# A four-layer block in fp32: the decay levels of two layers moved to one engine, their steps and a compression product placed anew

## The chip, the cores and the metric

One of the eight cores of a Trainium2 chip runs the whole program. The metric is the device time of one execution in microseconds; before, three runs gave a median of 1442.73 us (1440.99 to 1444.5). The core has five engines that work side by side and wait for each other by semaphores: TensorE (PE, with PEld for its weight loads), VectorE (DVE), ScalarE (ACT), GpSimd (POOL), and SyncE (SP), which only starts DMAs here.

## The reference, cut to what matters

The input is 256 tokens of 1024 features, all in fp32. Two layers of a first model (a recurrent one, a forgetting attention) are followed by two layers of a second, called layers 2 and 3 below, which the change touches. Such a layer does

```
proj = rms_norm(h) @ w_in                       # hq hf hi hg nq, six k/v of 128, 24 gates
o_hg  = hgrn2(hq, hf, hi, hg)                   # 4 heads of 128
o_nsa = gated sum of three attentions of 8 heads of 64 (2 key heads):
        compressed keys (15 blocks), "selected" and sliding-window
h += concat(o_hg, o_nsa) @ w_out
h += (silu(g) * u) @ w_ffn_out                  # g, u = rms_norm(h) @ w_ffn_in
```

With 256 tokens the selected and the window attention are both plain causal attentions. `hgrn2` needs, for each head, the sum over earlier tokens s of q_t * k_s * (product of the gates f between s and t), times v_s. The compressed keys and values are silu(window of 32 tokens @ w1) @ w2, for keys and for values.

## The kernel before

**Weights.** Every large product is a stream of units: 128 x 1024 values, 512 KB, loaded by SyncE into one of 8 `raw` buffers. ScalarE converts a unit to a high part `whi` (`splits`, line 939), VectorE subtracts it to get the low part `wlo` (line 1516), and TensorE forms each product as three matmuls, high x high, low x high, high x low (`products`, lines 277, 281, 282). There are 4 split buffers, so both engines run at most 3 units ahead (`AHEAD`). Where an engine does other work it first catches up: `full(name)` (lines 942 and 1519) does `splits(fills[name].pos + AHEAD)` and then waits for the PSUM bank; `pos` is the unit count when that bank's fill was closed. In VectorE's `soft`, `cap` limits this to what the next scores will allow.

**Banks.** PSUM has 8 banks. `fill(name, bank)` waits until the bank's previous fill was read, `close` signals that it is full, `read_out(name)` waits for its reader.

**Order.** It is written out by hand. In layers 2 and 3 the front is: block A and B (key and value rows), `hf` by feature, `hq` by feature, the `nq` block (queries of the attentions), with `rows_turned` (turned keys and queries) and first levels hung behind single units; then four units of `windows_by_unit(0)` (the compression's first product, for keys, bank 0) and the last turns. Then `attend` runs 12 steps. Step n of TensorE does, in this order:

```
between[n]; scores(n+1); weave; between[(n,1)]; turns(n); weave; between[(n,2)]; values(n-1)
```

A weave is half a unit of product from `side()`: `windows_by_unit(1)` (values, bank 1), then `hi` and `hg` (banks 0 and 1), 20 halves in all, so steps 10 and 11 have none. Turns go to bank 6. ScalarE's `soft` in step n does its `between[n]`, then `exps(n+1)` and then the copy of turn n out of bank 6. VectorE's `soft` in step n does the row maximum of scores n (line 1601, scaled at 1605; ScalarE's exps(n) waits for it), then its `between[n]`. A step has 4 heads in the first two steps of each attention and 2 heads in the other four.

**The levels.** The gate products between s and t are built by doubling. Level 0 is the diagonal (`level(0, half)`, `diagonal`). Level l (1 to 7) pairs blocks of 2^(l-1) tokens, level 8 the two halves of the sequence. Before, there are four arrays of 128 x 1024: F (prefix products of the gates within a block), S (suffix products), K and Q. GpSimd updates S and F for each level (lines 1488 and 1489); VectorE's `advance(l)` forms X from K*S and Q*F (lines 1984 and 1985); TensorE multiplies (`level`, lines 735, 751, 742, bank 7), and VectorE takes the result under a mask (`take`, line 1965). Levels 0 to 2 stand in the front, levels 3 to 8 in steps 0 to 5. `hgrn_out` multiplies the finished matrix with the values.

**The compression.** `hidden_in(kv)` (ScalarE) and `ch_silu(kv)` (VectorE, line 1994) apply silu and free the bank; `ch_turned` turns the result (bank 6), `cmp_keys_values` is the second product (lines 784 and 786, bank 6), GpSimd's `cmp_key_rows` normalises the keys, `cmp_keys_turned` turns them (bank 6); then `cmp_scores`, `cmp_exps`, `cmp_probs`, `cmp_out`, `cmp_add`.

Of the kernel before, what the change touches and what calls it, by code (L numbers as in the profile page):

```python
# [86 lines left out]
def program(nc, a):  # L87
    ctx = ExitStack()
    with ctx:
# [150 lines left out]
        def _(pe):  # L240
# [139 lines left out]
            def windows_by_unit(kv, flat):  # L380
# [3 lines left out]
                out = fill(name, kv)  # L384
# [328 lines left out]
            for L in (2, 3):  # L713
# [11 lines left out]
                def level(l, half=0):  # L725

                    q, kk, X = slot(8, 1024), slot(1, 1024), slot(9, 1024)
                    name = f"lev{L}.{l}"
                    if l == 0:
# [3 lines left out]
                        for h in range(4):  # L733
                            c = h * T + half * P
                            m = pe.matmul(out[:, h * P:(h + 1) * P], kk[:, c:c + P], q[:, c:c + P], start=True, stop=True)
# [4 lines left out]
                    if l == LEVELS:  # L740
                        for h in range(4):
                            m = pe.matmul(out[:, h * P:(h + 1) * P], X[:, h * T:h * T + P],
                                          X[:, h * T + P:(h + 1) * T], start=True, stop=True)
# [3 lines left out]
                    for tt in range(TT):  # L747
                        for h in range(4):
                            c = h * T + tt * P
                            q2 = X[:, c:c + P].rearrange("p (n two m) -> p n two m", two=2, m=s)[:, :, 1, :]  # L750
                            m = pe.matmul(out[:, (tt * 4 + h) * 64:(tt * 4 + h + 1) * 64], X[:, c:c + P], q2,  # L751
# [3 lines left out]
                def hgrn_out(tt):  # L755

                    if tt == 0:
                        for t in range(TT):
                            read_out(f"hi{L}.{t}")
                        read_out(f"lev{L}.{LEVELS}")  # L760
# [49 lines left out]
                def cmp_out(tt):  # L810
# [3 lines left out]
                    out = fill(f"co{L}.{tt}", 3)  # L814
# [17 lines left out]
                def side():  # L832

                    yield from windows_by_unit(0, flat)
# [12 lines left out]
                def rows_turned(groups):  # L847

                    for g in groups:
                        pe.wait_ge(ev("zrow"), 2 * i + (1 if g == 2 else 2))  # L850
                        for tt in range(TT):
# [4 lines left out]
                            turn(f"zT{L}.{tt}.{g}", (6, 3)[tt], tiles)  # L856
# [1401 lines left out]
```

## Time and profile before

| | us |
|---|---|
| median of 3 runs | 1442.73 |
| the profiled execution | 1444.79 |
| its span, first to last instruction | 1443.0 |
| TensorE busy | 1359.7 (94%) |
| VectorE busy | 880.3 (61%) |
| ScalarE busy | 714.2 (49%) |
| GpSimd busy | 192.4 (13%) |
| mean granted TensorE clock | 0.97 |

The profile is one execution. Busy is time in which an engine ran an instruction. The chain that ended last is 81% TensorE, 10% VectorE, 5% ScalarE. The granted clock is the share of TensorE's full clock (2.4 GHz) that it was given; 0.50 is 1.2 GHz. A releaser, in brackets behind a row, is what ended the idle time before it. Matmul rows overlap, since the engine is pipelined; what one costs is read from the distance of starts. Layer 2's front and attention lie at 656 to 834 us, layer 3's at 1048 to 1226.

### The profile page before, as it was taken

The numbers are of one execution on the slowest core, as the hardware profiler recorded it, in microseconds if no ns is written. First come the engines' busy times: TensorE is split into PE (matmuls) and PEld (weight loads), VectorE is DVE, ScalarE is ACT, GpSimd is POOL, SyncE is SP. The second block draws the span as 40 slices with busy tenths as digits, with TensorE's granted clock in tenths as the row PEclk, the third lists the DMA queues.
The fourth block names the chain that finished last, engine by engine and source line by source line (L and its number), as shares of the span: only waits on it lengthen the run. The fifth ranks groups of instructions, "written<-read, shape, count | busy, mean of one in ns | idle before, by whom it ended". The sixth has DMA issues, their size and how long they took to land.

```text
span 1443.0 us, 18641 instructions
## 1 busy us (share of the span) xinstructions
PE 1359.7 (94%) x7251; PEld 1152.2 (80%) x7251; DVE 880.3 (61%) x1136; ACT 714.2 (49%) x1167; POOL 192.4 (13%) x206
## 2 busy tenths in 40 slices
PE   7879999999988999999989899999999898999998
PEld 5657888878777888888977778888888776788887
DVE  4875665665534656557764556666577555566665
ACT  6464554454454545446443345555464444455553
POOL 2211000011530300002322010000023220100000
PEclk9989999998999999999979999999999799999999
DMA  9333655544522555545431135555454311355551
GB/s 364 136 117 117 233 174 207 188 152 158 177 72 71 178 203 178 202 159 195 160 118 59 59 117 204 190 176 183 155 194 158 117 59 44 131 190 179 199 194 56
DMA packets 62328, 224.44 MB, mean 156 GB/s; under 512 B 7192, under 2 KB 7328, under 8 KB 62240
## 3 DMA queue, kind: packets, MB, share of 16 engines
q1 hardware_dynamic: 59616, 214.23, 42.7%
q0 software_dynamic: 1904, 6.82, 1.5%
q10 hardware_dynamic: 720, 2.19, 0.4%
q8 instruction: 58, 0.95, 0.3%
q14 instruction: 30, 0.25, 0.1%
HBM read 222.16 MB, written 1.05 MB: 155 GB/s over the span
## 4 chain that ended last, share of the span: by engine, by line
PE 81%; DVE 10%; ACT 5%; issue 3%; POOL 2%; DMA 0%; POOLq 0%; DVEq 0%; ACTq 0%
PE ps L277 15%; PE ps L281 15%; PE ps L282 15%; PE ps L323 15%; PE ps L327 7%; PE ps L423 3%; PE ps L458 2%; PE ps L330 2%; PE ps L481 2%; DVE wlo L1516 2%; PE ps L751 1%; ACT scr L993 1%; PE ps L329 1%; DVE xn L1555 1%; DVE small L1601 1%
## 5 line engine op out<-in xcount | busy, mean ns | idle before, releaser
L1516 DVE TENSOR_TENSOR wlo<-raw,whi 128x1024 fp32r<-128x1024 f32 (+1 forms) x402 | 485.7, 1229 | 295.3 <-ACT whi L939 293.7
L939 ACT ACTIVATE whi<-raw 128x1024 fp32r<-128x1024 f32 (+1 forms) x409 | 424.3, 1048 | 332.9 <-PE ps L323 178.6
L323 PE MATMUL ps<-XT,whi 128*128 128x512 f32 x896 | 318.6, 399 | 0.0
L327 PE MATMUL ps<-XT,wlo 128*128 128x256 f32 x896 | 251.7, 281 | 0.0
L323 PEld LDWEIGHTS ps<-XT,whi 128*128 128x128 f32 x896 | 168.5, 188 | 41.0
L277 PE MATMUL ps<-whi,HT_hi 128*128 128x512 f32 (+1 forms) x496 | 189.9, 383 | 6.8 <-DVE wlo L1516 6.3
L282 PE MATMUL ps<-whi,HT_lo 128*128 128x512 f32 (+1 forms) x496 | 188.4, 380 | 0.0
L281 PE MATMUL ps<-wlo,HT_hi 128*128 128x512 f32 (+1 forms) x496 | 188.0, 379 | 0.0
L327 PEld LDWEIGHTS ps<-XT,wlo 128*128 128x128 f32 x896 | 169.4, 189 | 1.2
L277 PE MATMUL ps<-whi,XT 128*128 128x512 f32 (+2 forms) x352 | 143.1, 407 | 16.7 <-DVE wlo L1516 7.9
L281 PE MATMUL ps<-wlo,XT 128*128 128x512 f32 (+2 forms) x352 | 137.8, 391 | 0.0
L282 PE MATMUL ps<-whi,XT 128*128 128x512 f32 (+2 forms) x352 | 137.2, 390 | 0.0
L277 PEld LDWEIGHTS ps<-whi,HT_hi 128*128 128x128 f32 x496 | 94.9, 191 | 24.5 <-DVE wlo L1516 7.9
L282 PEld LDWEIGHTS ps<-whi,HT_lo 128*128 128x128 f32 x496 | 95.0, 192 | 17.3
L281 PEld LDWEIGHTS ps<-wlo,HT_hi 128*128 128x128 f32 x496 | 95.1, 192 | 16.9
L993 ACT ACTIVATE scr<-ps,small 128x256 f32<-128x256 f32 (+1 forms) x96 | 47.4, 501 | 112.8 <-DVE small L1605 99.0
L1336 POOL TENSOR_SCALAR small<-small 128x1 f32<-128x1 f32 x20 | 11.0, 550 | 660.0 <-ACT xn L976 659.8
L277 PEld LDWEIGHTS ps<-whi,XT 128*128 128x128 f32 x352 | 70.5, 200 | 35.2 <-DVE wlo L1516 11.1
L277 PE MATMUL ps<-whi,MX_hi 128*128 128x512 f32 x192 | 79.2, 413 | 15.2 <-issue 6.1
L282 PEld LDWEIGHTS ps<-whi,XT 128*128 128x128 f32 x352 | 70.6, 201 | 13.6
L281 PEld LDWEIGHTS ps<-wlo,XT 128*128 128x128 f32 x352 | 70.8, 201 | 10.1
L282 PE MATMUL ps<-whi,MX_lo 128*128 128x512 f32 x192 | 76.6, 399 | 0.0
(253 smaller groups left out, 1933.6 us busy)
## 6 DMA issues: line engine op xcount, KB each, us to landing
raw<-in_w_m SPq DMA_DIRECT2D x152, 512.0 KB, 4.2
raw<-in_w_n SPq DMA_DIRECT2D x108, 512.0 KB, 4.2
raw<-in_w_c SPq DMA_DIRECT2D x48, 512.0 KB, 4.0
raw<-in_w_o SPq DMA_DIRECT2D x32, 512.0 KB, 3.5
raw<-in_w_kv SPq DMA_DIRECT2D x16, 512.0 KB, 4.1
raw<-in_w_b SPq DMA_DIRECT2D x16, 512.0 KB, 3.2
raw<-in_w_w SPq DMA_DIRECT2D x16, 512.0 KB, 4.2
raw<-in_w_a SPq DMA_DIRECT2D x12, 512.0 KB, 8.2
```

The lines of the kernel that those rows point to most:

```text
L277: m = pe.matmul(out, xh, wh, start=first, stop=False)
L281: pe.matmul(out, xh, wl, start=False, stop=False)
L282: return pe.matmul(out, xl, wh, start=False, stop=last)
L323: m = pe.matmul(outs[f][:, :], hi[:, j, at], both, start=(k == 0), stop=False)
L327: pe.matmul(outs[f][:, 0:T], lo[:, j, at], XT[0][:, k, :], start=False, stop=False)
L330: m = pe.matmul(outs[f][:, :], hi[:, j, at], both, start=False, stop=True)
L423: m = pe.transpose(out[0:f, at:at + p], t, ident[0:p, 0:p])
L458: m = pe.matmul(out[:, j * klen:(j + 1) * klen], qT(h0 + j)[0:kd, tt * P:(tt + 1) * P], kT(h0 + j)[0:kd, 0:klen], start=(j == 0 or not cau ...
L481: m = pe.matmul(out[:, h * hd:(h + 1) * hd], turned(tag, n)[:, (j * kt + t) * P:(j * kt + t + 1) * P], V(h, t), start=(t == 0), stop=(t == ...
L939: act.activation(whi[:, g % NSPLIT, 0:w], raw[:, g % NRAW, 0:w], ACT.Copy).then_inc(split_hi, 1)
L993: m = act.activation(probs(tag, n)[:, j * klen:(j + 1) * klen], src, ACT.Exp, bias=sm(f"nmax{which}", 16)[:, c:c + 1], accum_out=sm(f"rsum ...
L1516: dve.tensor_tensor(wlo[:, g % NSPLIT, 0:w], raw[:, g % NRAW, 0:w], whi[:, g % NSPLIT, 0:w].bitcast(F32), ALU.subtract).then_inc(split_lo, 1)
```

## The change

It touches layers 2 and 3 alone.

1. GpSimd's level work goes (its loop, and S). VectorE keeps KS and QF in place of K, Q and X, and multiplies them in place: at level l, the first half of each pair of KS by the second block's whole gate product, the second half of QF by the first block's. The block products of the next level, `decay_of[l]`, half as many each time, are one more VectorE instruction behind `take`. The factor is one value per block, read as a broadcast.
2. The first product of the compression for the keys (four units) comes right behind `hf`, ahead of `nq` and `hq`; `nq` comes before `hq`; the turns of the queries hang behind units 2 and 3 of `hq`. No level is left in the front.
3. In the attention levels 0 to 8 stand in steps 0 to 7, each in a step of its own or at the other end of one; `hgrn_out` and others move later. VectorE's `advance(l+1)` stands in step l. Each `advance(l+1)` waits for level l to be in its bank.
4. Banks: `ch.1` goes to bank 3 (was 1), `zT` to 6 and 7 (were 6 and 3), `co.1` to 7 (was 3).
5. ScalarE's and VectorE's own orders follow.

The diff, cut to its core:

```diff
-                out = fill(name, kv)                      # windows_by_unit
+                out = fill(name, 3 * kv)
...
-                            turn(f"zT{L}.{tt}.{g}", (6, 3)[tt], tiles)
+                            turn(f"zT{L}.{tt}.{g}", 6 + tt, tiles)
...
                 feature_pairs(f"hf{L}", (4, 5), [a[w][u] for u in range(4)], {})
-                feature_pairs(f"hq{L}", (0, 1), [a[w][4 + u] for u in range(4)], {2: lambda: rows_turned((2,))})
-                block_of(f"nq{L}", w, 3, tok(XT), [2, 3], {1: lambda: level(0, 0), 2: lambda: level(0, 1), 3: lambda: level(1)})
-
                 pe.wait_ge(ev("xclo"), i + 1)
-                next(tiles_left)
-                next(tiles_left)
-                level(2)
-                next(tiles_left)
-                next(tiles_left)
-                rows_turned((0, 1))
+                for _ in windows_by_unit(0, flat):
+                    pass
+                block_of(f"nq{L}", w, 3, tok(XT), [2, 3], {1: lambda: rows_turned((2,))})
+                feature_pairs(f"hq{L}", (0, 1), [a[w][4 + u] for u in range(4)],
+                              {2: lambda: rows_turned((0,)), 3: lambda: rows_turned((1,))})
...
-                    {(0, 1): lambda: level(3),
-                     (1, 1): lambda: level(4),
-                     (2, 1): lambda: level(5), (2, 2): ch_turned,
-                     (3, 1): lambda: level(6), (3, 2): cmp_keys_values,
-                     (4, 1): lambda: level(7),
-                     (5, 1): lambda: level(8),
-                     (6, 2): lambda: (cmp_keys_turned(), hgrn_out(0)),
-                     7: lambda: cmp_scores(0), (7, 1): lambda: cmp_scores(1), (7, 2): lambda: hgrn_out(1),
-                     (9, 2): cmp_probs,
-                     (10, 1): lambda: cmp_out(0), (10, 2): lambda: cmp_out(1),
+                    {(0, 1): lambda: level(0, 0), (0, 2): lambda: level(0, 1),
+                     (1, 1): lambda: level(1), (2, 1): lambda: level(2), (3, 1): lambda: level(3), (4, 1): lambda: level(4),
+                     5: lambda: level(5), (5, 2): lambda: (level(6), cmp_keys_turned()), (6, 2): lambda: level(7),
+                     (2, 2): ch_turned, (3, 2): cmp_keys_values,
+                     7: lambda: cmp_scores(0), (7, 1): lambda: level(8), (7, 2): lambda: cmp_scores(1),
+                     (8, 1): lambda: hgrn_out(0), (8, 2): lambda: hgrn_out(1),
+                     10: cmp_probs, (10, 2): lambda: cmp_out(0), 11: lambda: cmp_out(1),
                      12: hgrn_rows}, (6, 6), weave)
...                                                        # ScalarE
                 first_in()
+                hidden_in(0)
                 turned_in((2,))
-                queries_in()
...
-                hidden_in(0)
                 turned_in((0, 1))
+                queries_in()
...
-                     {2: lambda: hidden_in(1), 3: ch_in, 4: cmp_in, 6: values_in,
-                      7: lambda: (copy_out(f"kcT{L}", ...), hgrn_in(0)),
-                      8: lambda: hgrn_in(1),
-                      9: cmp_exps,
-                      10: lambda: (gates_in(), copy_out(f"cpT{L}", ...))})
+                     {2: lambda: hidden_in(1), 3: ch_in, 4: cmp_in,
+                      6: lambda: (values_in(), copy_out(f"kcT{L}", ...)),
+                      9: lambda: (cmp_exps(), hgrn_in(0)),
+                      10: lambda: (copy_out(f"cpT{L}", ...), hgrn_in(1), gates_in())})
...                                                        # VectorE
+                decay_of = {1: F}
+                for l in range(2, LEVELS):
+                    decay_of[l] = S[:, 1024 - (2048 >> (l - 1)):1024 - (1024 >> (l - 1))]
...
+                    if l == 1:
+                        dve.tensor_tensor(QF, Q, F, ALU.mult).then_inc(ev("xlev"), 1)
+                        return
+                    f = fills[f"lev{L}.{l - 1}"]
+                    splits(f.pos + AHEAD)
+                    dve.wait_ge(bank_full[f.bank], f.turn)
                     if l <= LEVELS:
-                        m_ = 1 << (l - 1)
+                        m_ = 1 << (l - 2)
                         v = lambda t: t.rearrange("p (n two m) -> p n two m", two=2, m=m_)
-                        dve.wait_ge(ev("lev"), 8 * i + l)
-                        dve.tensor_tensor(v(X)[:, :, 0, :], v(K)[:, :, 0, :], v(S)[:, :, 0, :], ALU.mult)
-                        dve.tensor_tensor(v(X)[:, :, 1, :], v(Q)[:, :, 1, :], v(F)[:, :, 1, :], ALU.mult).then_inc(ev("xlev"), 1)
+                        G = decay_of[l - 1].rearrange("p (n two) -> p n two", two=2)
+                        if l > 2:
+                            dve.wait_ge(ev("decay_of"), (LEVELS - 2) * i + l - 2)
+                        dve.tensor_tensor(v(KS)[:, :, 0, :], v(KS)[:, :, 0, :], bc(G[:, :, 1], 2, m_), ALU.mult)
+                        dve.tensor_tensor(v(QF)[:, :, 1, :], v(QF)[:, :, 1, :], bc(G[:, :, 0], 2, m_),
+                                          ALU.mult).then_inc(ev("xlev"), 1)
+                    take(l - 1)
+                    if l < LEVELS:
+                        dve.tensor_tensor(decay_of[l], G[:, :, 0], G[:, :, 1], ALU.mult).then_inc(ev("decay_of"), 1)
...
                 decays()
-                queries()
-                advance(1)
-                diagonal(0)
-                diagonal(1)
-                advance(2)
+                ch_silu(0)
...                                                        # the query rows, then
-                ch_silu(0)
+                queries()
                 dve.wait_ge(ev("qrstd"), i + 1)
-                soft(tags, {0: lambda: advance(3), 1: lambda: advance(4),
-                            2: lambda: (advance(5), ch_silu(1)),
-                            3: lambda: (branch(1, 0), advance(6), cmp_values()),
-                            4: lambda: (advance(7), key_sums(), cmp_values_in()),
-                            5: lambda: advance(8), 6: lambda: advance(9),
-                            7: lambda: branch(1, 1),
-                            8: lambda: (cmp_scores(), hgrn_sums(0)),
-                            9: lambda: (branch(2, 0), cmp_probs(), hgrn_sums(1)),
-                            10: gates,
-                            11: lambda: (hgrn_rows(), cmp_add(0), cmp_add(1))})
+                soft(tags, {0: lambda: (advance(1), diagonal(0)), 1: lambda: (diagonal(1), advance(2)),
+                            2: lambda: (ch_silu(1), advance(3)),
+                            3: lambda: (cmp_values(), branch(1, 0), advance(4)),
+                            4: lambda: (advance(5), key_sums()),
+                            5: lambda: (advance(6), cmp_values_in()),
+                            6: lambda: advance(7),
+                            7: lambda: (branch(1, 1), advance(8)),
+                            8: lambda: (cmp_scores(), advance(9)),
+                            9: lambda: (cmp_probs(), branch(2, 0)),
+                            10: lambda: (hgrn_sums(0), hgrn_sums(1), gates()),
+                            11: lambda: (cmp_add(0), cmp_add(1), hgrn_rows())})
```

## Rows read from the trace of the kernel before

**Rows 1.** Windows by stage: length, then busy us (count) of PE, PEld, DVE, ACT, POOL, clock, DMA share, GB/s.

```profile
700.00:832.80 132.80, 118.21 (x699) 101.40 (x697) 75.86 (x117) 55.25 (x123) 29.51 (x29) 0.90 0.23 84
1092.00:1224.70 132.70, 118.84 (x701) 101.65 (x699) 76.14 (x118) 55.55 (x124) 29.49 (x29) 0.90 0.25 84
687.00:729.80 42.80, 38.93 (x268) 35.66 (x266) 30.93 (x34) 20.41 (x27) 12.18 (x7) 0.96 0.52 176
```

**Rows 2.** TensorE's timeline, where it had stood: start, us, instruction, [idle before, releaser].

```profile
72.39 0.50 PE L277 MATMUL ps<-whi,XT 128*128 128x512 f32 x1 [2.49 <-DVE wlo L1516]
...
723.15 0.38 PE L277 MATMUL ps<-whi,HT_hi 128*128 128x256 f32 x1 [2.59 <-DVE wlo L1516]
...
729.85 1.49 PE L458 MATMUL ps<-mixf 64*128 64x128 f32 x8 [1.25 <-ACT mixf L954]
...
753.00 0.77 PE L277 MATMUL ps<-whi,XT 128*128 128x512 f32 x1 [3.42 <-issue]
...
819.21 0.65 PE L423 MATMUL ps<-const,small 128*120 128x128 f32 x2 [3.53 <-ACT scr L954]
```

**Rows 3.** Windows again: behind the wait at 72.39, and layer 2's four low stretches.

```profile
72.40:78.40 6.00, 4.19 (x20) 3.00 (x20) 5.51 (x2) 5.51 (x8) 5.37 (x3) 1.00 0.25 87
723.60:727.00 3.40, 3.40 (x19) 3.11 (x17) 3.22 (x4) 1.84 (x3) 0.00 (x0) 0.50 0.78 273
...
730.40:737.30 6.90, 6.90 (x30) 5.92 (x28) 4.77 (x7) 2.12 (x9) 2.56 (x2) 0.51 0.05 20
750.90:761.10 10.20, 8.10 (x29) 7.31 (x30) 3.99 (x6) 2.75 (x6) 2.56 (x2) 0.50 0.37 137
819.20:826.10 6.90, 6.89 (x23) 5.48 (x23) 3.90 (x10) 2.20 (x7) 0.00 (x0) 0.51 0.22 78
```

**Rows 4.** TensorE's timeline through one step of the attention, at full clock.

```profile
772.83 1.13 PE L458 MATMUL ps<-mixf 64*128 64x256 f32 x4
...
774.11 0.40 PE L277 MATMUL ps<-whi,XT 128*128 128x512 f32 x1
...
775.50 1.89 PE L751 MATMUL ps<-scr 128*128 128x64 f32 x16
777.23 0.61 PE L423 MATMUL ps<-const,scr 128*128 128x128 f32 x4
...
779.07 1.00 PE L481 MATMUL ps<-scr 128*128 128x64 f32 x8
```

**Rows 5.** VectorE's timeline: single rows, and from 764.63 one step's work.

```profile
719.40 0.68 DVE L2120 TENSOR_TENSOR scr<-scr,mixf 128x512 f32<-128x512 f32 x1
...
742.84 1.80 DVE L1516 TENSOR_TENSOR wlo<-raw,whi 128x1024 fp32r<-128x1024 f32 x1
...
752.50 0.40 DVE L1994 SCALAR_TENSOR_TENSOR xn<-xn,ps 30x256 f32<-30x256 f32 x1
...
764.63 0.69 DVE L1984 TENSOR_TENSOR scr<-scr 128x512 f32<-128x512 f32 x1
...
765.84 0.71 DVE L1965 COPY_PREDICATED scr<-const,ps 128x512 f32<-128x512 uint32 x1
...
767.21 0.68 DVE L1601 TENSOR_REDUCE small<-ps 128x2 f32<-128x512 f32 x1
```

**Rows 6.** ScalarE's timeline behind that step, TensorE's answer, and exps of four heads.

```profile
768.28 0.56 ACT L993 ACTIVATE scr<-ps,small 128x256 f32<-128x256 f32 x1 [5.59 <-DVE small L1605]
...
769.38 1.05 ACT L939 ACTIVATE whi<-raw 128x1024 fp32r<-128x1024 f32 x1
770.32 0.59 ACT L954 ACTIVATE scr<-ps 128x512 f32<-128x512 f32 x1
...
771.06 0.38 PE L784 MATMUL ps<-w2c,small 128*30 128x64 f32 x4 [0.55 <-ACT scr L954]
...
783.14 0.46 ACT L993 ACTIVATE scr<-ps,small 128x128 f32<-128x128 f32 x1 [3.42 <-DVE small L1605]
...
784.89 1.06 ACT L939 ACTIVATE whi<-raw 128x1024 fp32r<-128x1024 f32 x1
```

More of the change, by code:

```diff
@@ L734, in level @@
                             c = h * T + half * P
-                            m = pe.matmul(out[:, h * P:(h + 1) * P], kk[:, c:c + P], q[:, c:c + P], start=True, stop=True)
+                            m = pe.matmul(out[:, h * P:(h + 1) * P], KS[:, c:c + P], q[:, c:c + P], start=True, stop=True)
                         close(f"{name}.{half}", m)
@@ L741, in level @@
                         for h in range(4):
-                            m = pe.matmul(out[:, h * P:(h + 1) * P], X[:, h * T:h * T + P],
-                                          X[:, h * T + P:(h + 1) * T], start=True, stop=True)
+                            m = pe.matmul(out[:, h * P:(h + 1) * P], KS[:, h * T:h * T + P],
+                                          QF[:, h * T + P:(h + 1) * T], start=True, stop=True)
                         close(name, m)
@@ L749, in level @@
                             c = h * T + tt * P
-                            q2 = X[:, c:c + P].rearrange("p (n two m) -> p n two m", two=2, m=s)[:, :, 1, :]
-                            m = pe.matmul(out[:, (tt * 4 + h) * 64:(tt * 4 + h + 1) * 64], X[:, c:c + P], q2,
+                            q2 = QF[:, c:c + P].rearrange("p (n two m) -> p n two m", two=2, m=s)[:, :, 1, :]
+                            m = pe.matmul(out[:, (tt * 4 + h) * 64:(tt * 4 + h + 1) * 64], KS[:, c:c + P], q2,
                                           start=True, stop=True)
@@ L759, in hgrn_out @@
                             read_out(f"hi{L}.{t}")
+                        read_out(f"lev{L}.{LEVELS - 1}")
+                    else:
                         read_out(f"lev{L}.{LEVELS}")
@@ L813, in cmp_out @@
                         read_out(f"cpT{L}")
-                    out = fill(f"co{L}.{tt}", 3)
+                    out = fill(f"co{L}.{tt}", (3, 7)[tt])
                     for half in range(2):
@@ L1298, in _ @@
                 soft([f"sl{L}", f"sw{L}"],
[L1299 to L1303 removed]
+                     {2: lambda: hidden_in(1), 3: ch_in, 4: cmp_in,
+                      6: lambda: (values_in(),
+                                  copy_out(f"kcT{L}", sm("kcT", 2 * NCMP)[0:64, :], lambda ps: ps[0:64, 0:2 * NCMP])),
+                      9: lambda: (cmp_exps(), hgrn_in(0)),
+                      10: lambda: (copy_out(f"cpT{L}", cpT[0:8 * NCMP, :], lambda ps: ps[0:8 * NCMP, 0:T]), hgrn_in(1),
+                                   gates_in())})
                 for n in ("hr", "nr"):
@@ L1456, in _ @@
                 rstd(sm("rk8k", 8), 8, 64, "krstd")
+                pool.wait_ge(ev("qsum"), i + 1)
+                rstd(sm("cq", 16), 16, 64, "qrstd", 0.125)
                 def cmp_key_rows():
@@ L1476, in cmp_key_rows @@
                     pool.tensor_tensor(kr[0:n30, 32:64], kr[0:n30, 32:64], kt_[0:n30, 32:64], ALU.add).then_inc(ev("kcr"), 1)
-                pool.wait_ge(ev("hfk"), i + 1)
-                pool.memset(S, 1.0).then_inc(ev("lev"), 1)
-                for l in range(1, LEVELS):
-                    m_ = 1 << (l - 1)
-                    Fv = F.rearrange("p (n two m) -> p n two m", two=2, m=m_)
-                    Sv = S.rearrange("p (n two m) -> p n two m", two=2, m=m_)
-                    tot = Fv[:, :, 1, m_ - 1]
-                    lastf = Fv[:, :, 0, m_ - 1]
-                    pool.wait_ge(ev("xlev"), 8 * i + l)
-                    chain(pool, "p_chain", pool.tensor_tensor(Sv[:, :, 0, :], Sv[:, :, 0, :], bc(tot, 2, m_), ALU.mult))
-                    pool.tensor_tensor(Fv[:, :, 1, :], Fv[:, :, 1, :], bc(lastf, 2, m_), ALU.mult).then_inc(ev("lev"), 1)
-                    if l == 2:
-                        pool.wait_ge(ev("qsum"), i + 1)
-                        rstd(sm("cq", 16), 16, 64, "qrstd", 0.125)
                 cmp_key_rows()
@@ L1940, in decays @@
                     step(m)
-                    dve.tensor_scalar(K, F, -0.5, 0.5, ALU.mult, ALU.add).then_inc(ev("hfk"), 1)
+                    step(dve.tensor_scalar(KS, F, -0.5, 0.5, ALU.mult, ALU.add))
                 def queries():
```

15 lines of the change are left out of this document (2 added, 13 removed).

## The prediction

> **What bounds the kernel now.** I read the windows by stage first. In the two stages that the change touches TensorE is busy for 118.2 of 132.8 us and 118.8 of 132.7, at a mean granted clock of 0.90 [rows 1]. So each layer loses time in two ways: 14.6 and 13.9 us with no matmul, and half of what is done at half clock. The windows on the low stretches of layer 2 show a clock of 0.50 with TensorE busy for 3.40, 6.90, 8.10 and 6.89 us; half of that, 12.6 us, is lost [rows 3]. Layer 3 repeats the pattern 392 us later. I put its low stretches at the same price: losses are 27.2 and 26.5 us, 53.7 together. Everything else there is matmul work, which the change only moves. So the question is which idle goes and which comes.
>
> Then I read TensorE's timeline for what ends its idle time [rows 2]. It stood 2.59 us before 723.15 for a split weight (VectorE was busy with the query rows), 1.25 us before the first scores for ScalarE's copies of the turned queries, 3.42 us before 753.00 and 3.53 us before 819.21 for ScalarE's copy out of bank 6. The 3.42 us has no releaser named: the product waits for bank 1, which `ch_silu(1)` at 752.50 frees [rows 5]. Each of these is followed by a low stretch.
>
> **The change, part by part.** Durations of TensorE at full clock, by differences of starts [rows 4]: one unit's half (a weave) 1.39; level 1.73; a turn and a weave together 1.84, so a turn 0.44; a scores step 1.28 to 1.4. Values and a level-0 half are eight matmuls to a level's sixteen: 0.87.
>
> *The front.* The window 687.0 to 729.8 is 42.8 us, of it 3.9 idle [rows 1], and 3.4 low (1.7 lost) [rows 3], and some 0.3 more lost around its edge. Moving four level products out takes 0.9 + 0.9 + 1.73 + 1.73 = 5.3 us. The 2.59 us wait goes: VectorE has only `ch_silu(0)` and the query rows there, and the splits it owes (three units of lead) are done while TensorE runs the nq and hq blocks, 22 us of products. The window product of four units takes 5.8 us and VectorE's splits 1.22 each beside `decays`, so its fourth unit comes some 0.6 late. The last turn is again right before attention, so the 1.25 us copy wait stays. First scores: 729.85 - 5.3 - 2.6 - 2.0 + 0.6, that is about 720.5. Loss in the front: 1.85 us, no low clock. The weight loads on SP's queue follow the new order of the units (four window units ahead of eight others); with the DMA engines at 0.23 of their time in this stage and 0.52 in the front [rows 1] and eight raw buffers ahead of the conversion, I cost that at nothing; if a load were late it would show as ScalarE waiting, up to one landing time.
>
> *VectorE's own work.* The two half-tile products of a level stay 0.61 us each from start to start [rows 5]; they are now done in place. That they read a broadcast operand costs nothing by the nearest row, L2120, 0.68 with one [rows 5]; I take 0.61 (bounds 0.61 and twice that; the row is the same shape, so the lower). The new decay products are 512, 256, 128, 64, 32 and 16 wide: the first is a row's 0.68 [rows 5], a smaller one lies between 0 and that; I take half, 0.3, for the two that follow and 0.15 for the rest. GpSimd's fourteen products go. They were never what TensorE waited for directly, but they stretched VectorE: the split at 742.84 took 1.80 against 1.22 for the same form [rows 5]. I use the undisturbed durations throughout.
>
> The Trainium skill, "SBUF — State Buffer", section "Who interferes with whom", says that a VectorE instruction with two SBUF inputs and a GpSimd instruction that reads SBUF shut each other out for the whole instruction. The stretched split agrees. By that rule the change gains on every level; with the stretched durations instead, each chain below would be some 0.6 us longer.
>
> *The chain of a step.* This is where it costs. `soft` on VectorE does reduce(n), then `between[n]`, then reduce(n+1); ScalarE does exps(n+1) before it copies turn n out of bank 6. Before, `advance(l)` in step n waited for a level computed one step earlier. After, `advance(n+1)` in step n waits for level n, which TensorE runs at (n,1) of that same step. Queued behind this new wait on VectorE is reduce(n+1), and for that ScalarE waits with exps(n+1), the next conversion and the copy of turn n. So whatever uses bank 6 at (n,2) waits for: two products 1.21, take 0.61, decay 0.3, reduce and scale 0.9, exps of two heads 1.10, split 0.94, copy and signal 0.74. The pieces are one run of rows, 764.63 to 771.06 (which has a 0.76 us copy L2002 in it and no decay) [rows 5, 6]: 5.9 us. TensorE has one turn and one weave to do meanwhile, 1.84. Two products sit there:
> - (2,2), `ch_turned`: VectorE must also do `ch_silu(1)` with a split ahead of it (the weight copy of the unit comes after `hidden_in(1)`), 1.3 us more. Idle 5.9 + 1.3 - 1.85 = 5.35 us.
> - (3,2), `cmp_keys_values`: idle 5.7 - 1.85, about 3.8 us.
>
> Before, that second place cost 0.55 [rows 6], and the first nothing. The 3.42 us is gone in exchange (`ch.1` is in bank 3 now).
>
> *Three smaller waits.* Level 1 needs bank 7 from `diagonal(1)`, whose `full` first splits two units that ScalarE converts only after exps(1). From the first scores: reduce(1) ends at +7.0, exps of four heads 1.75 [rows 6], conversion 0.95, copy 0.55, conversion 0.95, VectorE split 1.2, diagonal 0.6: +13.2, where TensorE is there at +10.9. Idle 2.35. At (5,2), `cmp_keys_turned`: from level 4's end VectorE and ScalarE need 13.5 us (level 5's products wait for a split), TensorE has 11.0 of work: 2.5. `hgrn_out(1)` follows `hgrn_out(0)` by one turn and weave, and needs ScalarE's `hgrn_in(0)`, now behind exps(9) and `cmp_exps`: 0.9. The turn of step 11 waits for `gates`, which waits for `hgrn_in(1)` and `gates_in`: 7.1 us of chain against 4.6 of work, 2.6. The old 3.53 before `cmp_probs` goes, since values(8) and two sums moved off that path.
>
> *Clock.* Both long waits will be followed by a low stretch. After 753.00 it lasted 8.1 us of work, after 819.21 6.9 [rows 3]; I take 7.3 each, 3.65 lost. For waits of 2.35 to 2.6 the rows disagree: 2.49 at 72.39 was followed by full clock [rows 2, 3], 2.59 at 723.15 by a low one. I take one of the three, at the mean of 1.7 and 3.4: 2.5.
>
> *Sum for a layer.* Idle 0.6 + 1.25 + 2.35 + 5.35 + 3.8 + 2.5 + 0.9 + 2.6 = 19.35; clock 7.3 + 2.5 = 9.8. Together 29.15, twice 58.3, against 53.7: 4.6 us slower. The profiled run took 1444.8 (span 1443.0), 2.1 above the median of 1442.73; added to the median it is 1447.3.
>
> **The rivals.**
> - *Only the two long waits lower the clock.* For it: 72.39. Against: 723.15. It takes 2 x 2.5 off: 1442.3, no change. Chance 0.20.
> - *Faster: the clock returns sooner.* Place: the work right behind (2,2) and (3,2), which is dense (scores, weave, level). If it is at half clock for only 3.4 us, as after 723.15 [rows 3], each costs 1.7 in place of 3.65, and the middle waits cost none: 2 x (3.9 + 2.5) = 12.8 less, 1434.5. It decides for faster as soon as a layer loses less than 5.9 us to the clock. For it: the first low stretch; against: three of four lasted 6.9 us or more. The same side is reached if the chain of a step is 1 us shorter than my rows (0.25 takes in both).
> - *Every middle wait lowers it:* 2 x 5 more, 1457.3; chance 0.10.
> - *The change doesn't do what it says:* the broadcast products take twice 0.61, or the small ones cost like wide ones. Each of the two bank-6 chains is then 1.2 to 1.5 longer: 5 to 6 us more, 1453. Chance 0.05.
> - The forecast itself: 0.40.
>
> **How the numbers follow.** The predicted time is the forecast's. The range leaves out the far end of the faster case and the dearest one: 1435 to 1456. Its own range is 1443 to 1452. No change means within 0.2% (2.9 us), about what a measurement of this kernel can tell. Faster is the second rival with a little of the first, 0.28; the same is most of the first and the lower edge of the forecast, 0.25; slower 0.47.
>
> **What would show it.** In the page after: no wait for VectorE's split before the last window units, and first scores at 720 to 721. In TensorE's timeline: an idle of 4 to 6 us before the 30x30 turns (L423, xn) and of 3 to 5 us before L784-type products with w2c, both ended by ScalarE's copy to scr. Low clock for about 7 us behind each. The GpSimd rows of 128x512 are gone and VectorE's split of 1.80 is back at 1.22. What would make it wrong: those two waits under 3 us, or full clock behind them; then the front's 7 us per layer is a plain gain.

## The result, and the profile after

Four runs of the changed kernel have a median of 1463.84 us (1462.87 to 1465.39), against 1443.34 us for the kernel before: a ratio of 1.0145, interval 1.0128 to 1.0163. The change makes the kernel 20.5 us slower. The forecast was 1447.3 us and its range ended at 1456: the direction was right, the size was not. The profiled execution took 1462.87 us with a span of 1461.0, at a mean clock of 0.961 (before 1443.0 and 0.970).

The page of the changed kernel, its part on busy time. The same 7251 matmuls keep TensorE busy for 9.9 us more, and GpSimd lost 30 instructions and 38 us:

```profile
PE 1369.6 (94%) x7251; PEld 1162.4 (80%) x7251; DVE 876.0 (60%) x1146; ACT 712.3 (49%) x1167; POOL 154.4 (11%) x176
```

Windows of the changed kernel, with the columns of [rows 1]: layer 2's attention, the seven stretches of low clock in layer 2, which answer to the four of [rows 3], and layer 3's attention, which answers to the second of [rows 1]:

```profile
697.00:837.50 140.50, 122.46 (x707) 107.09 (x706) 70.74 (x118) 51.73 (x121) 11.19 (x15) 0.85 0.22 73
...
719.50:723.00 3.50, 3.50 (x17) 3.43 (x17) 0.95 (x1) 1.72 (x8) 0.00 (x0) 0.51 0.00 0
733.00:737.00 4.00, 4.00 (x24) 4.00 (x23) 3.46 (x5) 0.00 (x0) 0.00 (x0) 0.57 0.23 84
746.50:757.50 11.00, 8.69 (x32) 7.12 (x32) 2.65 (x6) 2.44 (x7) 0.00 (x0) 0.53 0.15 48
764.00:774.50 10.50, 10.17 (x39) 8.49 (x39) 0.96 (x1) 0.51 (x3) 0.28 (x1) 0.51 0.16 50
787.50:798.50 11.00, 10.01 (x34) 8.49 (x35) 5.20 (x8) 5.17 (x15) 0.00 (x0) 0.53 0.17 48
804.50:808.50 4.00, 4.00 (x17) 3.53 (x17) 1.70 (x4) 2.15 (x5) 0.00 (x0) 0.57 0.00 0
835.50:839.50 4.00, 4.00 (x24) 4.00 (x23) 1.58 (x7) 1.40 (x3) 0.00 (x0) 0.57 0.00 0
1084.50:1225.00 140.50, 124.56 (x739) 110.18 (x737) 73.16 (x111) 53.48 (x114) 8.43 (x13) 0.85 0.28 94
```

Busy time by one minus the clock, row by row, is 1.7 + 1.7 + 4.1 + 5.0 + 4.7 + 1.7 + 1.7 = 20.6 us lost to the clock in the layer. Half-microsecond windows give 20.7 in each of the two layers; before they give 12.6 and 13.0.

TensorE's timeline of the changed kernel, every place from 687 us to layer 2's first output product where it stood over 0.2 us (columns as in [rows 2]):

```profile
688.82 0.39 PE L277 MATMUL ps<-whi,HT_hi 128*128 128x256 f32 x1 [0.55 <-DVE wlo L1496]
...
716.73 0.46 PE L458 MATMUL ps<-mixf 64*128 64x128 f32 x2 [1.14 <-ACT mixf L948]
...
731.47 0.30 PE L751 MATMUL ps<-scr 128*128 128x64 f32 x1 [2.27 <-DVE scr L1953]
...
748.81 0.39 PE L423 MATMUL ps<-const,xn 30*128 30x30 f32 x2 [4.78 <-ACT scr L948]
...
764.33 0.39 PE L786 MATMUL ps<-w2c,small 128*30 128x64 f32 x2 [3.96 <-ACT scr L948]
...
788.49 0.23 PE L423 MATMUL ps<-const,small 30*64 30x30 f32 x1 [2.35 <-ACT scr L948]
...
819.59 0.35 PE L769 MATMUL ps<-scr,xn 128*128 128x128 f32 x1 [0.89 <-ACT scr L948]
...
828.08 0.30 PE L423 MATMUL ps<-const,small 128*120 128x128 f32 x1 [0.21 <-ACT scr L948]
...
835.36 0.41 PE L423 MATMUL ps<-const,scr 128*128 128x128 f32 x2 [2.43 <-ACT scr L948]
...
841.02 0.47 PE L277 MATMUL ps<-whi,MX_hi 128*128 128x512 f32 x1 [0.84 <-DVE MX_lo L1521]
```

Set the two lists side by side: behind the waits of 1.14, 2.27, 4.78, 3.96, 2.35 and 2.43 us stands a low stretch each. Only the one at 804.5 has no wait in front. "Behind" is loose: the stretches at 746.5, 764 and 787.5 begin while TensorE still stands, the one at 733 begins 1.8 us and the one at 719.5 some 2.9 us after its wait has ended.

The difference lies in the two stages. From layer 2's first block to its first output product are 171.72 us before (662.22 to 833.94) and 182.28 after (658.74 to 841.02); in layer 3 171.37 and 182.24. That is 21.4 us more. Ahead of layer 2 the profiled run was 3.5 us quicker, in code that the change doesn't touch; the rest is the 18.0 us by which the spans differ. In layer 2 those windows hold 156.04 us of busy TensorE before and 162.85 after: of the 10.6 us more, 6.8 are busy time of the same products at a lower clock and 3.75 are idle.

VectorE and ScalarE of the changed kernel ahead of the 4.78 us wait (VectorE's timeline, then ScalarE's):

```profile
741.01 1.23 DVE L1496 TENSOR_TENSOR wlo<-raw,whi 128x1024 fp32r<-128x1024 f32 x1 [0.21 <-ACT whi L933]
742.15 0.40 DVE L1984 SCALAR_TENSOR_TENSOR xn<-xn,ps 30x256 f32<-30x256 f32 x1
742.48 0.67 DVE L1972 TENSOR_TENSOR scr<-scr 128x512 f32<-128x512 f32 x1
743.08 0.67 DVE L1973 TENSOR_TENSOR scr<-scr 128x512 f32<-128x512 f32 x1
743.69 1.27 DVE L1949 COPY_PREDICATED scr<-const,ps 128x512 f32<-128x512 uint32 x1
744.76 0.44 DVE L1977 TENSOR_TENSOR scr<-scr 128x256 f32<-128x256 f32 x1
745.14 0.67 DVE L1581 TENSOR_REDUCE small<-ps 128x2 f32<-128x512 f32 x1
```

```profile
746.04 0.56 ACT L987 ACTIVATE scr<-ps,small 128x256 f32<-128x256 f32 x1 [4.81 <-DVE small L1585]
...
747.13 1.05 ACT L933 ACTIVATE whi<-raw 128x1024 fp32r<-128x1024 f32 x1
748.08 0.59 ACT L948 ACTIVATE scr<-ps 128x512 f32<-128x512 f32 x1
```

This is how a bank is held: `ch_turned` needs bank 6 and nothing else that is late. The copy that frees it (L948) stands behind exps(3), which stands behind the maximum (L1581), which stands behind the level's four instructions (L1972, L1973, L1949, L1977), and these behind `ch_silu(1)` (L1984) and its split. The operand of `ch_turned` itself was ready at 742.55.

### The profile page after: what moved, and what is told of

It is laid out like the page before. It is cut to its first block, busy times and chain, and to the rows that moved or that the text cites. A ratio compares the mean times of both kernels' runs of the same rounds, so it can differ in the third digit from the quotient of the medians.

```text
span 1461.0 us, 18619 instructions
## 1 busy us (share of the span) xinstructions
PE 1369.6 (94%) x7251; PEld 1162.4 (80%) x7251; DVE 876.0 (60%) x1146; ACT 712.3 (49%) x1167; POOL 154.4 (11%) x176
## 3 DMA queue, kind: packets, MB, share of 16 engines
HBM read 222.16 MB, written 1.05 MB: 153 GB/s over the span
## 4 chain that ended last, share of the span: by engine, by line
PE 76%; DVE 12%; ACT 7%; issue 3%; POOL 2%; DMA 0%; DVEq 0%; POOLq 0%; ACTq 0%
PE ps L323 14%; PE ps L277 14%; PE ps L282 14%; PE ps L281 14%; PE ps L327 7%; DVE wlo L1496 3%; PE ps L423 2%; PE ps L330 2%; PE ps L458 2%; PE ps L481 2%; ACT scr L987 2%; ACT whi L933 1%; ACT scr L948 1%; PE ps L751 1%; DVE small L1581 1%
## 5 line engine op out<-in xcount | busy, mean ns | idle before, releaser
L277 PE MATMUL ps<-whi,XT 128*128 128x512 f32 (+2 forms) x352 | 144.2, 410 | 10.2 <-DVE wlo L1496 7.9
L282 PE MATMUL ps<-whi,XT 128*128 128x512 f32 (+2 forms) x352 | 139.3, 396 | 0.0
L281 PEld LDWEIGHTS ps<-wlo,XT 128*128 128x128 f32 x352 | 71.3, 203 | 10.8
```

Source lines behind the costliest of these rows:

```text
L277: m = pe.matmul(out, xh, wh, start=first, stop=False)
L281: pe.matmul(out, xh, wl, start=False, stop=False)
L282: return pe.matmul(out, xl, wh, start=False, stop=last)
```

## The experiments

Kernel 1 is that of experiment 1, and so on. Differences to the changed kernel are of medians; by the ratios to the kernel before they come out up to 1.4 us smaller, in experiment 8 1.3 us larger; for experiments 9 to 11 both are given. The kernel before had 1442.51 us beside the first four, 1442.14 beside the next four and 1440.63 beside the last three. Clock lost is worked out as above, from half-microsecond windows, for layer 2 and then layer 3.

**1. Other bank for the two products that stood longest.** Changed kernel, with

```diff
-turn(f"chT{L}", 6,
+turn(f"chT{L}", 7,
-out = fill(f"kvc{L}", 6)
+out = fill(f"kvc{L}", 7)
```

> The kernel after, with the compression's turn (ch_turned) and its second product (cmp_keys_values) in bank 7 in place of bank 6, so that neither waits for exps(n+1) and the copy of turn n. Theory A (the two long waits, 4.78 and 3.95 us of idle a layer, and the low clock behind them, 4.2 and 4.9 us, come from bank 6): the first wait falls to about 1.4 us (take(2) has to free bank 7), the second to about 0.3, and the low stretches behind them go; some 15 us a layer, 1434 us. Theory B (the chain level n, reduce(n+1), exps(n+1) sets the pace of a step anyway, so the wait only moves to turns(n+1) or to level(n+1)): at most 3 us a layer, 1458 us or more, with idle before the next turn in its place.

Measured: 1436.49 us (1434.14 to 1439.0), ratio 0.9964 (0.9949 to 0.998). TensorE's timeline of this kernel at the two places:

```profile
745.35 0.21 PE L423 MATMUL ps<-const,xn 30*128 30x30 f32 x1 [1.05 <-DVE scr L1949]
...
754.99 0.27 PE L786 MATMUL ps<-w2c,small 128*30 128x64 f32 x2 [0.31 <-DVE scr L1949]
```

The waits fell from 4.78 and 3.96 to 1.05 and 0.31, 7.4 us a layer, and the clock lost from 20.7 to 13.6. That is 14.5 us a layer, 29 in all, where the medians differ by 27.4: two bank numbers carry more than the whole loss. The two waits were for the bank, not for the data.

**2. The same waits, but with TensorE busy in them.** Changed kernel, with 19 products nobody reads ahead of `ch_turned` and 15 ahead of `cmp_keys_values`, into bank 3:

```diff
+for _ in range(n):                      # n = 19, then 15
+    pe.matmul(PS[3][:, :], XT[0][:, 0, 0:P], ...)
```

> The kernel after, with 19 extra products of 128x512 (4.45 us at full clock) ahead of the turn at (2,2) and 15 (3.5 us) ahead of the second product at (3,2), into a bank that is free; they only fill the two long waits and their results are used by nothing. Theory A (the low clock is the answer to these two waits): both low stretches go, their 4.2 + 4.9 us a layer come back, the chain itself is as long as before: 1464 - 18 = 1446 us. Theory B (the low clock follows from the kind of work, the scores with 64 rows and the turns, whatever stood before it): the stretches stay, 1464 us.

Measured: 1446.13 us (1443.28 to 1448.06), ratio 1.0028 (1.0013 to 1.0043). TensorE's timeline at the first place shows the stretch filled (L777), and the windows over both stretches that had been low show full clock:

```profile
746.46 4.49 PE L777 MATMUL ps<-XT 128*128 128x512 f32 x19
```

```profile
746.50:757.50 11.00, 10.82 (x64) 8.97 (x63) 4.84 (x11) 2.91 (x7) 0.00 (x0) 1.00 0.24 89
741.00:782.00 41.00, 38.42 (x236) 32.55 (x234) 20.70 (x38) 13.93 (x35) 4.10 (x11) 1.00 0.21 65
```

The useful products still wait for the same copies; yet the kernel is 17.7 us faster. Clock lost is 10.2 and 13.6 us, 17.6 less than the changed kernel's 41.4. So it was TensorE's standing still that brought the low stretches behind these waits, and they cost as much (8.8 us a layer) as the two waits themselves (8.7).

**3. The change's bank for the values' product, alone.** Kernel before, with `out = fill(name, 3 * kv)` in place of `fill(name, kv)`.

> The kernel before, with the second window product (ch.1) in bank 3 in place of bank 1, and nothing else: the one part of the change that takes away the 3.42 us wait at (2,0). Theory A (that bank conflict costs its idle and the low clock behind it, 4.1 us): 7 us a layer, 1429 us. Theory B (the idle moves to the turn at (2,2), which needs the same ch_silu(1)): less than 3 us a layer, 1438 us or more.

Measured: 1439.25 us (1432.41 to 1444.87), ratio 0.9985 (0.9965 to 1.0004): no change. B. The 3.42 us wait is gone, but TensorE now comes earlier to work that VectorE sets; and the clock still loses 13.0 us in layer 2 (10.2 in layer 3), at other places (timeline, then windows, of this kernel):

```profile
742.45 0.29 PE L751 MATMUL ps<-scr 128*128 128x64 f32 x1 [0.81 <-DVE scr L1965]
...
755.89 0.27 PE L423 MATMUL ps<-const,xn 30*128 30x30 f32 x2 [1.64 <-ACT scr L954]
```

```profile
792.00:802.50 10.50, 10.50 (x40) 8.94 (x39) 4.31 (x8) 2.74 (x6) 0.00 (x0) 0.51 0.14 50
```

That last stretch has no wait in it, and a wait of 1.19 us 5.5 us in front.

**4. VectorE alone, order and banks of before.** Changed kernel's `advance` and `decay_of`, with the front, the order of the attention and the banks of the kernel before.

> The change's levels alone: VectorE's in-place products and its decay products in place of GpSimd's, but the order of TensorE, ScalarE and VectorE and the banks as in the kernel before. Theory A (the move between engines costs nothing on TensorE's path; the loss is all in the placing): 1443 us, within 3. Theory B (VectorE's six more products a layer, or the chain through them, cost): over 1447 us.

Measured: 1445.91 us (1438.4 to 1451.27), ratio 1.0026 (0.9998 to 1.0053). It lies at A's edge: taking the levels from GpSimd costs 3.4 us with an interval from nothing to 7.6, and in no reading the 20.5. The median hides two groups of five runs: 1438.4 to 1443.09 us at mean clocks of 0.970 to 0.977, and 1448.74 to 1451.27 at 0.962 to 0.967. So this part alone costs nothing or some 8 us, and the difference between the groups is clock; why one kernel has both was not looked into. The order and the banks make the loss.

**5. All three compression products in bank 3.** Changed kernel, with `chT`, `kvc` and `kcT` in bank 3, whose earlier users are read long before.

> The kernel after, with three uses of bank 6 moved to bank 3, which is empty between ch_silu(1) and cmp_scores: the compression's turn, its second product, and the turn of the compressed keys. Theory A (each wait is a bank held by ScalarE's late copy): the three waits of 4.78, 3.95 and 2.36 us a layer all fall under 0.3, and the low clock behind them goes; against bank 7 for two of them (1436.5 us) another 3.7 us of idle and 2 to 3 of clock a layer: 1425 us. Theory B (the step's chain takes over as soon as bank 6 is out of the way): new idle before turns or levels, 1434 us or more.

Measured: 1420.0 us (1416.74 to 1421.15), ratio 0.9842 (0.9814 to 0.9869). All three waits are gone. The window from 740 to 783.5 us, over the places of all three, has full clock and 0.6 us of idle:

```profile
740.00:783.50 43.50, 42.91 (x284) 36.94 (x284) 27.89 (x51) 18.89 (x50) 4.47 (x11) 1.00 0.26 83
```

Clock lost: 10.2 and 6.8 us. Idle before: 4.78 + 3.96 + 2.35 - 0.59 = 10.5 us a layer less. Together 45 us in the profiles; 43.8 in the medians. That is 5 us under A's 1425: against kernel 1 the clock gave back 5.1 us a layer, not 2 to 3.

**6. Two more waits taken out.** Kernel 5, with VectorE's `full` of the diagonal splitting one unit ahead and no more, and `gates()` of VectorE moved from step 10 to step 11:

```diff
-ps = full(f"lev{L}.0.{tt}")
+ps = full(f"lev{L}.0.{tt}", 1)
-10: lambda: (hgrn_sums(0), hgrn_sums(1), gates()),
-11: lambda: (cmp_add(0), cmp_add(1), hgrn_rows())})
+10: lambda: (hgrn_sums(0), hgrn_sums(1)),
+11: lambda: (gates(), cmp_add(0), cmp_add(1), hgrn_rows())})
```

> As the one with bank 3, and two orders on VectorE: diagonal() no longer first splits units that ScalarE has not converted, and gates() moves from step 10 to step 11, behind the row maximum of step 11. Theory A (the waits of 2.3 us before level 1 and 2.4 us before the turn of step 11 come from these orders): both under 0.7 us, with some clock: 1415 us. Theory B (their idle moves on to level 2 and to the turned rows of hgrn): within 2 us of the one with bank 3.

Measured: **1407.66 us** (1406.55 to 1411.84), ratio 0.9765 (0.9736 to 0.9794). This version beats both kernels: 34.5 us under the one before, 56.2 under the changed one. Its layer 2 from 697 us to the end of the turns is 115 us of nearly unbroken work, and one low stretch is left (windows of this kernel):

```profile
697.00:812.20 115.20, 110.97 (x726) 96.86 (x724) 70.04 (x113) 53.04 (x122) 11.56 (x15) 0.97 0.30 101
778.00:785.00 7.00, 7.00 (x23) 5.58 (x23) 3.47 (x7) 2.15 (x5) 0.00 (x0) 0.51 0.21 75
```

The wait of level 1 is gone; the one of the last turn is 0.99 in place of 2.43, where A had under 0.7, and the time is 7 us under A's. Layer 3 has two low stretches, at 1153.5 and 1187.6. The wait of 1.14 us ahead of the first scores is unchanged, and the clock stays full behind it.

**7. TensorE busy in six waits.** Changed kernel, with idle products in six waits of a layer (4, 8, 19, 15, 9 and 9 of them).

> The kernel after, with extra products of 128x512 in six waits a layer: 4 before the first scores, 8 before level 1, 19 and 15 before the two long ones, 9 before the turn of the compressed keys, 9 before the turn of step 11; nothing uses their results. They end just before the wait does. Theory A (every one of these waits, the short ones too, is what lowers the clock): nearly all of the 20.7 us a layer comes back, 1464 - 40 = 1424 us. Theory B (only the two long ones do; the other low stretches stand where they stand for another reason): 1446 us, as with these two filled.

Measured: 1438.0 us (1435.34 to 1440.25), ratio 0.9968 (0.9954 to 0.9982), between the two. Clock lost is 3.4 and 6.8 us in place of 20.7 twice, 31 us less, and the time fell by 25.8. The filling itself cost next to nothing: in layer 2 the four products ahead of the first scores ended 0.25 us behind the copy waited for (719.44 and 719.19), the other five groups ended before theirs. But 1.45 us of wait was left ahead of `ch_turned`: from level 1 to there this kernel takes 17.22 us (732.89 to 750.11) and the changed kernel 17.34, though the latter's low stretch at 733 is gone. VectorE and ScalarE set that piece, and the clock given back there only lengthened the wait. It bears A's mechanism out and not its full sum. Even here a window without a wait is low:

```profile
791.00:798.50 7.50, 7.50 (x28) 6.08 (x28) 3.78 (x7) 2.15 (x5) 0.00 (x0) 0.54 0.13 51
```

**8. The old front.** Changed kernel, with the front's order of before (`hq`, `nq`, then the window units and the turns) on all engines; the levels stay in the attention.

> The kernel after, with the front of the kernel before: hq, then nq, then the four window units, then the turns of the queries; the levels stay in the attention. It undoes the second part of the change alone. Theory A (the early window product is what took away the wait for VectorE's split): a wait of 2 to 3 us comes back before the last window units, with 1.7 us of clock: 8 us slower than the kernel after, 1472 us. Theory B (moving three levels and their VectorE work out of the front did that by itself): the same time as the kernel after, 1464 us.

Measured: 1474.84 us (1474.27 to 1477.15), ratio 1.023 (1.0198 to 1.0261). The split that [rows 2] show late is late again, and TensorE's timeline has it standing longer for it:

```profile
715.68 0.38 PE L277 MATMUL ps<-whi,HT_hi 128*128 128x256 f32 x1 [3.27 <-DVE wlo L1496]
```

So the second part of the change gains 11.0 us by itself, and the rest costs 31.5; the change's 20.5 is the difference. The clock does not answer this wait as A had it. In layer 2 the 3.27 us are followed by full clock up to 734.7, over two more waits of 1.13 and 2.28; in layer 3 the same wait, before 1122.53, has a low stretch behind it (windows of this kernel):

```profile
716.00:734.50 18.50, 14.75 (x112) 12.99 (x111) 9.85 (x13) 9.70 (x25) 0.00 (x0) 1.00 0.42 142
1123.80:1127.20 3.40, 3.40 (x18) 2.53 (x17) 2.40 (x3) 1.89 (x5) 0.00 (x0) 0.50 0.90 281
```

**9 to 11. The price of one wait.** Kernel 6 has few waits, so one was put back at a time: `chT` in bank 6 (9), `kcT` in bank 6 (10), the diagonal's `full` splitting two units ahead (11). One line each.

> The version with the keys' compression chain in bank 3 (1407.7 us, no wait over 1.14 us in the attention) with one wait put back: ch_turned at (2,2) in bank 6 again, so it stands some 4.8 us per layer for ScalarE's late copy. A (a wait is followed by a low stretch, so it costs its length and 3.4 to 4.2 us of clock): 2 x 8.2 to 9.0 more, 1424 to 1426. B (the clock's losses come from the mix of work, not from this wait): 2 x 4.8 more, 1417. Where low stretches that stand elsewhere move or go, the result lies between.

> The same version with one middle wait put back: cmp_keys_turned at (5,2) in bank 6 again, some 2.35 us per layer. A (a middle wait too lowers the clock, by 1.7 to 4.8 us): 2 x 4.1 to 7.2 more, 1416 to 1422. B (idle alone): 2 x 2.35 more, 1412.4. Since a low stretch of 7 us without a wait stands close by in this version, the two may fall together: then B's number with A's mechanism.

> The same version with the other middle wait put back: VectorE splits two units ahead of the diagonal again, so that level 1 stands 2.28 us per layer in step 1. No low stretch is near in this version. A (a middle wait lowers the clock, for 3.5 to 7.5 us of work as in the changed kernel and in its variants): 2 x 4.0 to 5.7 more, 1415.7 to 1419. B (idle alone): 2 x 2.28 more, 1412.2.

Measured: 1426.73 us (1426.02 to 1429.28), 1416.0 (1414.99 to 1417.5) and 1416.54 (1414.43 to 1418.61). For each of the three, TensorE's timeline at the wait put back, and the window on the low stretch at it. Kernel 9:

```profile
745.12 0.28 PE L423 MATMUL ps<-const,xn 30*128 30x30 f32 x1 [6.28 <-ACT scr L948]
```

```profile
741.00:758.50 17.50, 13.38 (x48) 11.46 (x49) 6.33 (x15) 2.90 (x7) 0.00 (x0) 0.51 0.15 53
```

Kernel 10:

```profile
767.28 0.18 PE L423 MATMUL ps<-const,small 30*64 30x30 f32 x1 [2.39 <-ACT scr L948]
```

```profile
769.00:773.00 4.00, 4.00 (x15) 3.10 (x14) 1.66 (x5) 1.45 (x7) 0.00 (x0) 0.57 0.43 124
```

Kernel 11:

```profile
732.47 0.30 PE L751 MATMUL ps<-scr 128*128 128x64 f32 x1 [2.28 <-DVE scr L1953]
```

```profile
733.00:740.00 7.00, 7.00 (x36) 7.00 (x36) 3.79 (x6) 0.44 (x1) 0.00 (x0) 0.51 0.25 76
```

| kernel | wait, us | more than kernel 6, per layer, by medians | by ratios | per us of wait |
|---|---|---|---|---|
| 9 | 6.28 | 9.5 | 10.7 | 1.5 to 1.7 |
| 10 | 2.39 | 4.2 | 5.1 | 1.7 to 2.1 |
| 11 | 2.28 | 4.4 | 5.5 | 1.9 to 2.4 |

The two columns differ because the kernel before was quicker beside these three than beside kernel 6 (medians 1440.63 and 1442.14 us).

By the medians the last two are A's: a wait of 2.3 us costs about 4.3 (in kernel 10 a wait of 0.60 us of kernel 6 went at the same time). In the ninth the wait itself was mis-sized, 6.28 us where 4.8 was expected: with level 1's wait gone TensorE came earlier to a place that VectorE sets. What it costs beyond its length, 3.2 us, is just under A's lower end. The profiles agree for two of them: clock lost over both layers is 10.2 us in kernel 6, 16.8 in 9 and 13.6 in 10. In kernel 11 it is 10.2 again. There a low stretch follows the wait in both layers, but further on kernel 6's 7 us stretch has shrunk to 4 us in layer 2, is two of 4 us in layer 3, and its last one, at 1187.6, is gone; the spans differ by 3.8 us (1413.8 and 1410.0), the medians by 8.9. The mean clocks of all four runs of each kernel decide between these. One minus the clock, times the span, is 25.4 us in kernel 6's profiled run and 21.1 in each of its other three; in kernel 11 it is 24.0 in the profiled run and 29.8, 26.9 and 24.0 in the others (each to 0.7 us, since the clock is known to 0.001). The means are 22.2 and 26.2: 2.0 us of clock a layer, which with the 2.28 us of wait makes 4.3. The pair of profiles compared kernel 6's dearest run with one of kernel 11's two cheapest.

## Why the prediction was right about the direction and wrong about the size

**The front: right.** No wait for the split before the last window units but 0.55 us (0.6 worked out). First scores at 716.73 us; with the 3.5 us by which this execution was ahead when the layer began, 720.2, where 720.5 was worked out. The copy wait of 1.25 us [rows 2] stayed, at 1.14. Kernel 8 puts the gain of this part at 11 us, 5.5 a layer: 2.7 of it is the longer wait for the split, and 2.0 and 2.3 are what the clock loses more in that kernel's layers (22.75 and 23.0 us), not all of it behind this wait.

**VectorE's own work: right.** The products in place with a broadcast operand take 0.67 us and start 0.60 apart, as [rows 5] had it for the old form; the decay products 0.73, 0.44 and 0.28 us at 512, 256 and 128 wide (0.68, 0.3 and 0.3 worked out). Kernel 4 shows that this part is worth little: at most 8 us in one group of its runs, nothing in the other. GpSimd's work had stretched VectorE's splits: before, two of those of 128x1024 between 739 and 756 us take 1.80 and 1.75; in the changed kernel all between 723 and 764 take 1.23. Kernel 4 isolates it, since it keeps the order of before and lacks GpSimd's products: its splits there take 1.22 and 1.23. That agrees with the Trainium skill, "SBUF — State Buffer", section "Who interferes with whom", which the prediction weighs.

**The chain of a step: right.** Its waits held one by one:

| place | idle worked out | idle measured |
|---|---|---|
| last window units | 0.6 | 0.55 |
| first scores | 1.25 | 1.14 |
| level 1 | 2.35 | 2.27 |
| (2,2) `ch_turned` | 5.35 | 4.78 |
| (3,2) `cmp_keys_values` | 3.8 | 3.96 |
| (5,2) `cmp_keys_turned` | 2.5 | 2.35 |
| `hgrn_out(1)` | 0.9 | 0.89 |
| turn of step 11 | 2.6 | 2.43 |
| sum | 19.35 | 18.4 |

Experiments 1 and 5 confirm the cause too: another bank, and the waits are gone (in kernel 1 all but 1.05 and 0.31 us). Inside the sums not every term held. At (2,2) the split and `ch_silu(1)` reach only 0.45 us past the start of the turn that follows level 2 (742.03, 742.48) where 1.3 was added, and the masked copy takes 1.07 from start to start where 0.61 was taken; the two errors partly cancel, which is luck. The seven terms for level 1 add up to 13.0, not 13.2, an idle time of 2.1; the low stretch ahead of it delayed both sides of that race by 1.5 us, so the wait of 2.27 came out close all the same.

**The clock: this step failed.** It reads "I take 7.3 each, 3.65 lost" for the two long waits (the mean of its 8.1 and 6.9 is 7.5), and for the three of 2.35 to 2.6 us "I take one of the three, at the mean of 1.7 and 3.4: 2.5", 9.8 us in all. Measured are 20.7 us in each layer. The two long waits lost 4.1 and 5.0 us. The three middle ones were followed by low stretches all three times, at 1.7, 4.7 and 1.7 us. The 1.14 us ahead of the scores, which I had priced at its length, was followed by one of 1.7, and one more of 1.7 stands without a wait. By my terms: 1.8 more for the long waits, 5.6 for the middle ones, 3.4 for the two I had not counted. That is 10.8 of clock a layer too little, and 1.0 of idle too much. Twice 9.8 is 19.6; the median misses the forecast by 16.5. The rest is in the rule that half of the busy time is lost: products of 128x256 start 0.21 us apart in the low stretch at 720 and 0.12 at full clock, 1.8 times and not twice, and layer 2 grew by 10.6 us where lost clock and idle by that rule grew by 8.2 + 3.75.

The failure was in the reading of [rows 2 and 3]. I weighed one wait of 2.49 us at 72.39, followed by full clock, as much as the one at 723.15, followed by low. But the row at 72.39 comes from another stage, and the window read behind it stops at 78.40. The next one, over a wait of 2.96 us ahead of 80.29, is low (window of the kernel before):

```profile
78.50:85.30 6.80, 5.01 (x12) 3.97 (x13) 6.73 (x7) 3.09 (x4) 0.00 (x0) 0.50 0.55 175
```

In the stage that the change touches every wait over 2.5 us (2.59, 3.42, 3.53) had a low stretch behind it, and one of the three of 1.2 to 1.4 us had one too, the very wait ahead of the scores that I left at its length. The rival "every middle wait lowers it" (1457.3, given 0.10) had the mechanism, and still fell short by 6.5 us since it left the long waits and the short one as they were. The others fell: "only the two long waits" by the five low stretches elsewhere; "the clock returns sooner" needed less than 5.9 us lost a layer, and the broadcast products cost what was taken.

**What stays open.** Why a stretch is low where no wait stands (804.5 in the changed kernel, 792 in kernel 3, 778 in kernel 6, 791 in kernel 7) was not settled. And an equal wait is not always answered alike: the 1.14 us ahead of the first scores was followed by low clock in the changed kernel and in layer 2 of kernel 1, and by full clock in layer 3 of kernel 1 and in kernels 2, 5, 6, 9, 10 and 11; the 3.27 us of kernel 8 by full clock in layer 2 and low clock in layer 3. So that the 1.14 us caused the stretch 2.9 us behind it is not shown.

## What to carry to other kernels

A bank is free only when its reader has read it, and the reader stands in its engine's own queue: before moving work between steps, write down for each use of a bank what its reader's engine does ahead of the read, and give a late product a bank whose reader is early (here three numbers turned a change that lost 1.5% into a gain of 1.6%). Count a stop of TensorE of 2 to 6 us at one and a half to two and a half times its length, with a range in which a single one can pass unpunished, as the 3.27 us of kernel 8 did in one layer; take the rate from all stops of the same stage, not from one row elsewhere, and read on until the clock has changed or the next stop comes. Where a wait can't be avoided, products that nobody needs are cheaper than standing still (17.7 us here), but another bank for the same two uses gave 9.6 us more.

## What the runs showed of the hardware that was not expected

- Waits of 2.27 to 2.43 us were followed by 3.5 to 10 us of products at 1.2 GHz, three out of three in both layers of the changed kernel, and likewise in every other kernel that had a wait of 2.2 to 2.5 us there. A wait of 1.14 us was followed by low clock in some kernels and not in others, one of 3.27 us in one layer and not in the other (experiment 8). Products without a use in the waits kept the clock full over 41 us (experiment 2).
- Low stretches of 4 to 13.5 us also stood where TensorE did not stop, at the steps with the 64-row scores and the narrow compressed scores (64x15); in one version the loss there was 5.1 us (10.5 us, experiment 3), in another 6.8 us (13.5 us from 789.5, experiment 4).
- Taking one wait out or putting one back also moved low stretches further on (experiments 3 and 11). In kernel 11 one profile against one put the clock's part at nothing, the mean clocks of four runs each at 2.0 us a layer.
- The masked copy of levels 1 and 2 takes 1.27 to 1.30 us where those of higher levels take 0.70 or 0.71, at the same shape (changed kernel, layer 2).
